# Gate weights side by side in one stationary matrix, and the scores' stores cut up, in a hybrid GLA / Gated DeltaNet trunk

## The reference

```python
def gdn_mixer(h, w_in, conv_w, a_log, dt_bias, head_norm, w_out):
    proj = h @ w_in
    qkv, z, beta_logit, a_logit = split(proj)        # the last two: 8 columns each, one per head
    qkv = silu(causal_depthwise_conv(qkv, conv_w))
    q, k, v = split(qkv); q = l2_norm(q) * NDK ** -0.5; k = l2_norm(k)
    beta = sigmoid(beta_logit)
    log_a = -exp(a_log) * softplus(a_logit + dt_bias)
    o = run_segments(gdn_chunk_scan, 0, q, k, v, beta, log_a)   # meta tokens, then chunks of 64
    o = rms_norm(o, head_norm) * silu(z)
    return o @ w_out

def gdn_chunk_scan(q, k, v, beta, log_a, s0, c):
    g = cumsum(log_a) in each chunk
    m = strictly lower part of (beta k) k^T * exp(g_i - g_j)
    u, w = solve (1 + m) [u w] = [beta v, beta k exp(g)]
    a_qk = q k^T * exp(g_i - g_j)
    for each chunk:  v_new = u - w S;  o = (q exp(g)) S + a_qk v_new;  S = S exp(g_last) + k_dec^T v_new
```

## Time and profile before

| | |
|---|---|
| median of three executions | 1465.19 us (1463.52 to 1466.24) |
| the profiled execution | 1463.95 us, its span 1462.2 us |
| PE | 1425.5 us busy, 97% of the span |
| VectorE (DVE) | 762.5 us, 52% |
| ScalarE (ACT) | 461.6 us, 32% |
| GpSimd (POOL) | 419.0 us, 29% |
| transfers | 200.35 MB, 137 GB/s over the span |

### The profile page before, as it was taken

How to read it: one execution, slowest core, us unless ns; L and a number is a source line. 1 busy time by engine, 2 the same in 40 slices (tenths; PEclk the granted TensorE clock), 3 DMA queues, 4 the chain that set the end, 5 groups by cost and what they waited for, 6 DMA issues and landing times.

```text
span 1462.2 us, 21408 instructions
## 1 busy us (share of the span) xinstructions
PE 1425.5 (97%) x8458; PEld 1198.3 (82%) x8458; DVE 762.5 (52%) x937; ACT 461.6 (32%) x957; POOL 419.0 (29%) x358
## 2 busy tenths in 40 slices
PE   7999999999999999999999999999989999999997
PEld 5777799978888888999999999978867767777776
DVE  5223622234444356645645698789944654444442
ACT  4332731133222243333344533421232631111121
POOL 3212043442101121212211167243442441222210
PEclk9999999999999999999999999999999999999999
DMA  5521244476444224444454222336368895555530
GB/s 193 175 87 36 80 131 147 146 254 209 158 159 163 75 58 116 128 107 111 112 155 160 84 80 74 92 92 178 115 210 231 247 233 146 148 148 159 166 87 29
DMA packets 213918, 200.35 MB, mean 137 GB/s; under 512 B 62873, under 2 KB 177065, under 8 KB 213570
## 3 DMA queue, kind: packets, MB, share of 16 engines
q1 hardware_dynamic: 207234, 187.53, 43.0%
q10 hardware_dynamic: 6592, 11.54, 2.9%
HBM read 131.93 MB, written 67.09 MB: 136 GB/s over the span
## 4 chain that ended last, share of the span: by engine, by line
PE 53%; DVE 6%; ACT 2%; DMA 2%; issue 1%; SPq 1%; DVEq 0%; POOLq 0%; ACTq 0%; POOL 0%
PE banks L2157 17%; PE banks L2955 12%; PE banks L2224 12%; DVE gdn L2476 4%; PE banks L2051 2%; PE banks L3044 2%; PE banks L3011 2%; PE banks L3016 2%; PE banks L2075 1%; PE banks L3025 1%; DMA gdn<-gdn_v 1%; PE banks L2999 1%; DMA gdn_z<-gdn 1%; PE banks L2968 1%; ACT gdn L2302 1%
## 5 line engine op out<-in xcount | busy, mean ns | idle before, releaser
L2157 PE MATMUL banks<-hn_hi,gdn 128*128 128x352 f32 x1488 | 300.5, 327 | 0.0
L2157 PEld LDWEIGHTS banks<-hn_hi,gdn 128*128 128x128 f32 x1488 | 242.1, 188 | 4.8 <-issue 3.1
L2476 DVE SCALAR_TENSOR_TENSOR gdn<-gdn,conv_taps,gdn 128x1040 f32<-128x1040 f32 x96 | 175.9, 1832 | 13.6 <-ACT gdn L2288 10.8
L882 PE MATMUL banks<-gdn,hn_hi 128*128 128x512 f32 x528 | 168.1, 400 | 4.0 <-POOL gdn L604 3.1
L2224 PE MATMUL banks<-gdn,hn_hi 128*128 128x512 f32 x512 | 163.8, 400 | 1.8 <-ACT gdn L2423 1.4
L2428 POOL TENSOR_TENSOR gdn<-gdn,gdn 128x1024 fp32r<-128x1024 f32 x31 | 87.1, 2810 | 270.3 <-ACT gdn L2263 270.3
L2157 PE MATMUL banks<-hn_lo,gdn 128*128 128x352 f32 x744 | 158.2, 321 | 0.0
L2157 PEld LDWEIGHTS banks<-hn_lo,gdn 128*128 128x128 f32 x744 | 125.6, 188 | 0.0
L882 PEld LDWEIGHTS banks<-gdn,hn_hi 128*128 128x128 f32 x528 | 99.2, 190 | 28.8 <-ACT gdn L434 3.9
L2224 PEld LDWEIGHTS banks<-gdn,hn_hi 128*128 128x128 f32 x512 | 96.2, 190 | 29.1 <-issue 3.1
L882 PE MATMUL banks<-gdn,hn_lo 128*128 128x512 f32 x264 | 104.5, 396 | 0.0
(11 more groups left out here) (315 smaller groups left out, 2286.4 us busy)
## 6 DMA issues: line engine op xcount, KB each, us to landing
gdn<-in_gdn_w_in SPq DMA_DIRECT2D x32, 512.0 KB, 4.1
gdn<-in_x SPq DMA_DIRECT2D x16, 512.0 KB, 4.1
gdn<-in_gla_w_in SPq DMA_DIRECT2D x32, 256.0 KB, 4.7
gdn_kq<-gdn SPq DMA_DIRECT2D x16, 512.0 KB, 3.8
gdn_v<-gdn SPq DMA_DIRECT2D x16, 512.0 KB, 3.5
...
```

What stands on the lines that cost most here:

```text
L882: mm = pe.matmul(out_bank(g, u, i), h_[:, kt, k], piece_of(w_, q), start=(kt == 0 and e == 0), stop=(kt == KT - 1 and e == 2))
L2157: last = pe.matmul(a[:, b, 0:m], w[n % 2][:, kt, :], x[:, kt, PAD + s:PAD + s + m], start=(kt == 0 and e == 0), stop=(kt == KT - 1 and e = ...
L2476: dve.scalar_tensor_tensor(cv[:, :], xs[:, tap:tap + L], T.cw[:, tap, t:t + 1], cv[:, :], ALU.mult, ALU.add).then_inc(S("ni_conv"), 1)
```

## The change

**The gate tile.** Its low weights stand in the same matrix as the high ones: high in columns 0 to 39, low in columns 64 to 103. One matmul of 104 columns with `hn_hi` gives high x high in rows 0 to 39 and low x high in rows 64 to 103 of the bank; a second one, of 40 columns, adds high x low with `hn_lo`. So there are two matmuls for each row block and span, 48 in all. The two groups of rows are now added: ACT copies rows 64 to 103 to SBUF (`gate_low`), DVE adds rows 0 to 39 to them (`gate_logs`), and max, min and the exponential of `beta_logit` read the sum in SBUF, 1040 tokens at a time.

**The stores.** The meta tokens' systems are weighed before the last steps of the inversion, stored and loaded again at once. When the systems are done (`ni_u` 3), SP stores those of chunks 0 and 1 (`gdn_ua`, 8 partitions each), issues the meta loads, stores the other 14 chunks in one DMA for each head, loads chunk 0's part and chunk 1's decays, and only then waits for the whole store and loads the keys. The scan's buffers are laid out anew so that `St`, `ua`, `h[1]` and `vn` lie behind `sc`.

```diff
@@ tail of layer 0 (PE)
-                H.products(pe, GATE, [0], range(2))
+                H.products(pe, GATE, [0], range(3))
                 norm_out(s, None)
-                H.products(pe, GATE, [0], range(2, KT))
+                H.products(pe, GATE, [0], range(3, KT))
                 H.products(pe, GATE, [1])
@@ gdn_ahead
+GL = 64
-    g_hi = A.at(LATE + 5152, [P, KT, GW], F32R)
-    g_st = A.at(LATE + 5152 + KT * GW, [P, KT, GW])
-    g_lo = A.at(LATE + 5152 + 2 * KT * GW, [P, KT, GW], F32R)
+    g_w = A.at(LATE + 5152, [P, KT, P], F32R)
+    g_raw = A.at(LATE + 5152, [P, KT, P])
+    g_hi, g_lo, g_st = (g_[:, :, c:c + GL].rearrange("p k (a b) -> p k a b", b=A0)[:, :, :, 0:NH]
+                        for g_, c in ((g_w, 0), (g_w, GL), (g_raw, GL)))
     def product(pe, n, kt, e, b):
-        w = ((hi, hi, lo), (g_hi, g_hi, g_lo))[n][e]
+        if n:
+            c = GL + GW if e == 0 else GW
+            return pe.matmul(H.bank[:, 3 * n + b, :][0:c, 0:m], g_w[:, kt, 0:c], x[:, kt, PAD + s:PAD + s + m],
+                             start=(kt == 0 and e == 0), stop=(kt == KT - 1 and e == 1), skip_group_check=True)
@@ tile 3 (PE)
-                    pe.wait_ge(S("ni_min"), 3)
-                    pe.wait_ge(S("ni_ebeta"), 3)
+                    pe.wait_ge(S("ni_gsum"), 3)
@@ ACT
+            def gate_low():
+                act.wait_ge(S("ni_mm"), GATE + 1)
+                for b, (s, m) in enumerate(SPANS):
+                    act.activation(gate[:, s:s + m], acc[1][GL:GL + GW, b, 0:m], ACT.Copy).then_inc(S("ni_ebeta"), 1)
             def gate_exps():
-                for b, (s, m) in enumerate(SPANS):
-                    act.activation(be[:, s:s + m], acc[1][0:NH, b, 0:m], ACT.Exp, scale=-1.0).then_inc(S("ni_ebeta"), 1)
+                act.wait_ge(S("ni_gsum"), 3)
+                act.activation(be, be, ACT.Exp, scale=-1.0).then_inc(S("ni_ebeta"), 1)
@@ DVE
             def gate_logs():
                 for b, (s, m) in enumerate(SPANS):
-                    dve.tensor_scalar(mx[:, s:s + m], acc[1][A0:A0 + NH, b, 0:m], dt[:, 0:1], 0.0, ALU.add, ALU.max)\
-                       .then_inc(S("ni_max"), 1)
-                for b, (s, m) in enumerate(SPANS):
-                    dve.tensor_scalar(ax[:, s:s + m], acc[1][A0:A0 + NH, b, 0:m], dt[:, 0:1], 0.0, ALU.add, ALU.min)\
-                       .then_inc(S("ni_min"), 1)
+                    dve.wait_ge(S("ni_ebeta"), b + 1)
+                    dve.tensor_tensor(gate[:, s:s + m], acc[1][0:GW, b, 0:m], gate[:, s:s + m], ALU.add)\
+                       .then_inc(S("ni_gsum"), 1)
+                dve.tensor_scalar(mx, gate[A0:GW, :], dt[:, 0:1], 0.0, ALU.add, ALU.max).then_inc(S("ni_max"), 1)
+                dve.tensor_scalar(ax, gate[A0:GW, :], dt[:, 0:1], 0.0, ALU.add, ALU.min).then_inc(S("ni_max"), 1)
                 dve.tensor_tensor(ax, mx, ax, ALU.subtract).then_inc(S("ni_abs"), 1)
@@ the end of layer 1's first half (SP)
-            sp.wait_ge(S("ni_u"), 4)
+            sp.wait_ge(S("ni_u"), 1)
             sp.dma_start(T.gdn_uam, m_rows).then_inc(S("ni_uam_out"), 16)
-            sp.dma_start(T.gdn_ua, sc[:, 0:2 * C * C].rearrange("p (j x) -> p j x", x=2 * C)).then_inc(S("ni_ua_out"), 16)
+            sp.wait_ge(S("ni_uam_out"), 16)
+            meta_ahead(sp)
+            sp.wait_ge(S("ni_u"), 3)
+            for c in range(2):
+                sp.dma_start(T.gdn_ua.rearrange("(g c) j x -> c g (j x)", c=NCH)[c], sc[c::NCH, 0:2 * C * C]).then_inc(S("ni_uam_out"), 16)
+        def store_ua(sp):
+            for h in range(NH):
+                rows = slice(h * NCH + 2, (h + 1) * NCH)
+                sp.dma_start(T.gdn_ua[rows], sc[rows, 0:2 * C * C].rearrange("p (j x) -> p j x", x=2 * C)).then_inc(S("ni_ua_out"), 16)
@@ the scan (SP)
-            sp.wait_ge(S("ni_uam_out"), 16)
             load_meta()
+            F.store_ua(sp)
+            F.ua_first(sp)
+            load_ua(0)
+            load_ek(1)
+            F.ua_stored(sp)
             load_kt(0)
             load_kt(1)
-            sp.wait_ge(S("ni_ua_out"), 16)
-            load_ua(0)
-            load_ek(1)
```

More of the change, by code:

```diff
@@ L1750, in load_weights @@
         sp.wait_ge(E("gd_zero"), 1)
-        sp.dma_start(g_st[:, :, 0:NH], wv[:, :, c_gate:c_gate + NH]).then_inc(E("gd_gw_in"), 16)
-        sp.dma_start(g_st[:, :, A0:GW], wv[:, :, c_gate + NH:c_gate + 2 * NH]).then_inc(E("gd_gw_in"), 16)
+        for a in range(2):
+            sp.dma_start(g_raw[:, :, GL + a * A0:GL + a * A0 + NH], wv[:, :, c_gate + a * NH:c_gate + (a + 1) * NH])\
+              .then_inc(E("gd_gw_in"), 16)
     def load_next(sp, tile):
@@ L1769, in high @@
         act.wait_ge(E("gd_gw_in"), 32)
-        act.activation(g_hi[:, :, :], g_st[:, :, :], ACT.Copy).then_inc(E("gd_hi"), 1)
+        act.activation(g_hi, g_st, ACT.Copy).then_inc(E("gd_hi"), 1)
     def zero(pool):
-        pool.memset(g_st[:, :, :], 0.0).then_inc(E("gd_zero"), 1)
+        pool.memset(g_w[:, :, :].bitcast(F32), 0.0).then_inc(E("gd_zero"), 1)
     def low(pool):
-        for n, (l_, s_, h_) in enumerate(((lo, st, hi), (g_lo, g_st, g_hi))):
+        for n, (l_, s_, h_) in enumerate(((lo[:, :, :], st[:, :, :], hi[:, :, :]), (g_lo, g_st, g_hi))):
             pool.wait_ge(E("gd_hi"), n + 1)
-            pool.tensor_tensor(l_[:, :, :], s_[:, :, :], h_[:, :, :].bitcast(F32), ALU.subtract).then_inc(E("gd_lo"), 1)
+            pool.tensor_tensor(l_, s_, h_.bitcast(F32), ALU.subtract).then_inc(E("gd_lo"), 1)
     def product(pe, n, kt, e, b):
-        w = ((hi, hi, lo), (g_hi, g_hi, g_lo))[n][e]
         x = (H.hn_hi, H.hn_lo, H.hn_hi)[e]
         s, m = SPANS[b]
-        return pe.matmul(H.bank[:, 3 * n + b, :][0:(P, GW)[n], 0:m], w[:, kt, :], x[:, kt, PAD + s:PAD + s + m],
+        if n:
+            c = GL + GW if e == 0 else GW
+            return pe.matmul(H.bank[:, 3 * n + b, :][0:c, 0:m], g_w[:, kt, 0:c], x[:, kt, PAD + s:PAD + s + m],
+                             start=(kt == 0 and e == 0), stop=(kt == KT - 1 and e == 1), skip_group_check=True)
+        w = (hi, hi, lo)[e]
+        return pe.matmul(H.bank[:, 3 * n + b, :][:, 0:m], w[:, kt, :], x[:, kt, PAD + s:PAD + s + m],
                          start=(kt == 0 and e == 0), stop=(kt == KT - 1 and e == 2))
@@ L1792, in products @@
             for kt in rows:
-                for e in range(3):
+                for e in range(H.parts[n]):
                     product(pe, n, kt, e, b)
     H.load_weights, H.load_small, H.high, H.zero, H.low = load_weights, load_small, high, zero, low
-    H.product, H.products = product, products
+    H.product, H.products, H.parts = product, products, (3, 2)
     H.st, H.load_next = st, lambda sp: load_next(sp, wv[:, :, NQK:NQK + P])
@@ L1833, in gdn_in @@
         ax, mx, g, be = (sc[0:NH, n * L:(n + 1) * L] for n in range(4))
+        gate = sc[0:GW, 3 * L:4 * L]
         cm, cwn = H.cm, H.cwn
@@ L1900, in col, with sync @@
             return 2 * NQK + v_of(n) * P
-        def sync(sp, ahead):
+        def sync(sp, ahead, meta_ahead):
             def load(n):
@@ L2363, in window @@
                 if n - 1 == GATE:
+                    gate_low()
                     gate_exps()
@@ L2681, in vector @@
             ev_v(NV // P - 1, 2)
+            weigh_meta()
             for _ in inverse:
@@ L2724, in gdn_scan @@
         behind.end = ahead.end
-        St = behind.take([P, NH, NDV])
         oT_hi = behind.take([P, KO, P], F32R)
         oT_lo = behind.take([P, KO, P], F32R)
-        kq_at, ek_at, St_at = 0, 2 * NH * 2 * C, ahead.end
+        og = [behind.take([P, HP, NDV]) for n in range(2)]
+        h0 = behind.take([P, D])
+        kt = [behind.take([P, HP, NDK]) for n in range(2)]
+        assert behind.end <= FRONT + 2 * C * C
+        behind.end = FRONT + 2 * C * C
+        vn = behind.take([P, HP, NDV])
+        kq_at, ek_at, St_at = 0, 2 * NH * 2 * C, behind.end
+        St = behind.take([P, NH, NDV])
+        ua = [behind.take([P, HP, 2, C]) for n in range(2)]
+        h = [h0, behind.take([P, D])]
         last_hi = A.at(St_at, [P, KO, P], F32R)
         last_lo = [A.at(n, [P, KO // 2, P], F32R) for n in (kq_at, ek_at)]
-        og = [behind.take([P, HP, NDV]) for n in range(2)]
-        vn = behind.take([P, HP, NDV])
-        kt = [behind.take([P, HP, NDK]) for n in range(2)]
-        ua = [behind.take([P, HP, 2, C]) for n in range(2)]
-        h = [behind.take([P, D]) for n in range(2)]
         junk = T.hn_hi_f32[:, :, D:TP]
@@ L2801, in sync_ahead, with sync_meta @@
             sp.dma_start(hnw[:, :], head_norm).then_inc(S("ns_in_hnw"), 16)
+        def sync_meta(sp):
+            for p in range(2):
+                sp.dma_start(um[RM[p], :, :], T.gdn_uam.rearrange("(h p) j i -> p j h i", p=2)[p])\
+                  .then_inc(S("ns_in_m"), 16)
         def sync(sp):
@@ L2850, in load_meta @@
             def load_meta():
-                for p in range(2):
```

(10 more changed lines are left out.)

20 lines of the change are left out of this document (14 added, 6 removed).

## The result

The changed kernel takes 1479.47 us, the median of four executions (1477.92 to 1481.02), beside 1464.36 us for four of the kernel before: ratio 1.0105, 95% interval 1.0084 to 1.0127. It is slower by some 15 us. The forecast was 1466.2 with a range up to 1469.5, and it was wrong. The profiled execution took 1480.1 us with a span of 1478.2.

The account below looks back on a forecast made before the run. PE, busy 97% of the span, was taken as the bound. Terms -2.5 + 0 + 1.35 + 1.7 + 1.3 = +1.85 on 1463.95 gave 1465.8; 0.4 added for clock luck made 1466.2 us, range 1460.0 to 1469.5.

Parts of the forecast that it names:

- 16 products in the tail: Layer 0's tail: 16 fewer gate matmuls at 0.157 us each bring the barrier 2.5 us sooner.
- 8 products behind the barrier: Gate's span 2: 8 fewer matmuls gain 0, since PE waits there for POOL's low weights, then for SiLU, instead.
- The gate's chain: Gate's values on DVE and ACT: copies and sums delay the chain to PE's SiLU wait before tile 2's transposes, +1.35 us.
- The clock behind the longer wait: After PE's SiLU wait before tile 2's transposes, grown to 3.2 us, the clock drops: +1.7 us, bounds 0 and +1.7.
- The stores: End of z: the bulk store ends later and holds z's stores, ACT's evictions and PE: +1.3 us, bounds +0.1 and +3.
- eight packets on the same engines, 8 x 1.29 us: Bulk store: if every 14-partition DMA starts with the same engines, these carry 8 packets, 10.3 us, ending at 1086.7.
- The third: Slower rival, 1085 to 1096: store ends 3 us later, 1.6 to 3.2 us more half clock; 1469 to 1470.7; chance 0.20.
- The first rival: End of z: z's stores get through, PE's waits and the half clock go, -6.1 instead of +1.3: 1458.8; chance 0.13.
- The second: Rival: gate's chain costs only +0.3, the clock holds, stores at +0.1: 1461.9 to 1462.5; chance 0.10.

Follow-up runs that it names:

- the run with columns: Changed kernel, two first stores left out, bulk as eight DMAs of all 128 partitions and an eighth of their columns each: 1463.22 us.
- the gate's part alone: Kernel before with only the gate's change (48 products, copies, sums), stores and layout as before: 1464.47 us, ratio 0.9999.
- the two runs with 16 partitions to a DMA: Changed kernel without the two first stores, bulk as eight DMAs of 16 partitions: neighbouring ones 1482.45 us, ones 8 apart 1472.43 us.
- the run with neighbours: Changed kernel, two first stores left out, bulk as eight DMAs of 16 neighbouring partitions, a whole head each: 1482.45 us, ratio 1.0123.
- the run with 1 KB packets: Kernel before with the gate's part, store in its old place as two DMAs of all 128 partitions, even and odd 1 KB pieces: 1466.42 us.

## Why the prediction was wrong, step by step

**16 products in the tail, -2.5: right.** PE restarted behind the barrier 8.11 us after DVE's drain began (518.51 - 510.4) and now 5.63 after it (513.33 - 507.7): 2.5. The wide matmuls start 0.157 us apart:

```profile
510.32 0.32 PE L1790 MATMUL banks<-hn_hi,gdn 128*104 128x344 f32 x1
510.47 0.32 PE L1790 MATMUL banks<-hn_lo,gdn 128*40 128x344 f32 x1
510.63 0.32 PE L1790 MATMUL banks<-hn_hi,gdn 128*104 128x344 f32 x1
```

**8 products behind the barrier, 0: right.** PE waits 1.20 us for POOL in their place, and 1.10 for SiLU.

**The gate's chain, +1.35: right in size (+1.5), not in its detail.** The difference on DVE ended 5.1 us after the first copy began, as forecast; but ACT's copies came behind the split at 529.49 and the three sums ran with them, while POOL held nobody for long (1.05 us for the max).

**The clock behind the longer wait, +1.7: right as a mechanism, too small, and a matter of chance.** In the changed kernel it cost 2.5 us. Windows of the changed kernel:

```profile
514.00:518.00 4.00, 4.00 (x18) 4.00 (x17) 0.29 (x1) 0.00 (x0) 1.35 (x2) 0.59 0.52 137
...
550.00:555.00 5.00, 4.71 (x19) 4.65 (x20) 0.80 (x2) 1.20 (x4) 0.00 (x0) 0.50 0.39 105
```

With a wait of 3.36 us the clock stayed at 1.00 in the run with columns and in the gate's part alone, and fell in the two runs with 16 partitions to a DMA. In the run with neighbours:

```profile
548.62 0.66 PE L2076 MATMUL banks<-consts,gdn 128*128 128x128 f32 x4 [3.36 <-ACT gdn L2326]
550.00:555.00 5.00, 5.00 (x26) 4.88 (x26) 1.40 (x3) 2.11 (x4) 1.18 (x1) 0.71 0.32 86
```

In the other seven profiled kernels with the chain the wait was 3.46 to 4.16 us, and the clock fell each time. With waits of 1.85 to 2.02 us, in the three without it, it never fell there. What was not forecast: the gap at the barrier (2.23 us in every kernel) also let the clock fall, in 7 of the 14 profiled kernels. It cost 1.55 us in six of them and 2.9 in the run with 1 KB packets. The kernel before had shown it whole, once, and I took that for its state. Such drops may be part of why a kernel's runs scatter by up to 9 us; no run isolates them.

**The stores, +1.3 with bounds +0.1 and +3: wrong, and this alone made the forecast wrong.** Measured: +15.4. The step that failed is "eight packets on the same engines, 8 x 1.29 us": it took from the earlier trace rows that a packet of 32.7 KB takes 1.29 us, and counted only how the packets spread over the engines. That count was right as far as the trace shows: the first DMA of the bulk has 14 large packets in flight together. But the earlier trace rows are of a DMA whose 16 packets in flight come from partitions spread over all 128. The bulk's packets took 2.6 us in the mean, and those of its first DMA 4.3 to 5.2 but for two. Eight at 2.6 are 21 us instead of 10.3, and the bulk lasted 29 us, from 1083.6 to 1112.5. The rest of the 29 us is z's packets and stretches in which an engine had none of the bulk: from 1084 to 1104 SP's queue kept 67.5% of the 16 engines busy and z's 17.9%. In the kernel before the store's packets ended at 1086.6, 1.3 us later than the prediction read from its rates; that changes little. Even the upper bound of 3 us kept to 1.29 us a packet.

A second size in the same term was off as well: the two stores and four loads ahead of the bulk took SP 7.1 us (1075.19 to 1082.26) where the prediction had 2.8. That alone is not the loss. The run with 16 neighbours has no first stores and issued its bulk at 1074.47, and lost as much.

**The rivals.** The third had the place (1085 to 1096), the mechanism (the store ends later and z's last places come free later) and the sign, and priced it at 3 us of delay and 1.6 to 3.2 of half clock, well under half of what came, because it used the same 1.29 us. The half clock behind the gap did not grow with it. The first rival (z's stores get through) was half true: z's packets did get more turns than in the earlier trace rows, 1.09 MB in 20 us, and that did not help, since each store still took some 18 us to land. The second (the chain costs little, the clock holds) did not come: the chain cost 1.5 us and the clock fell.
